# A retrieval kernel's second attention in two query groups, the second between the gathers; GpSimd adds a quarter of the gathered rows

## The reference

```python
# x: (512, 1024); ctx: (256, 1024); both normed and modulated -> h, hc; u = h @ w_in
q = rms_norm(u[:, :256]) @ w_uq                 # 16 heads of 64 + 32 (rotary) features
k, v = split(rms_norm([u; uc][:, 256:384]) @ w_ukv)   # 768 keys: 512 tokens + 256 of the context
y_a = softmax(q k^T * 96**-0.5) v @ w_o_mla
y_c = conformer_conv(u)                         # 31 taps, layer norm, silu, pointwise
x = x + g1 * ((gate_a * y_a + gate_c * y_c) @ w_out)
h2 = modulate(rms_norm(x), sh2, sc2)
# per token and each of 8 heads: top 16 of 128 x 128 experts by product keys
hidden = gelu(u_experts[e] . h2)                # e: 8 * 16 = 128 experts for each token
x = x + g2 * sum(gate * hidden * v_experts[e])
out = rms_norm(x)
```

## Time and profile before

| what | us |
|---|---|
| median of 3 runs | 3001.97 (2996.91 to 3003.27) |
| the profiled execution's own time | 3003.84 |
| its span in the profile | 3002.5 |
| TensorE busy | 2639.8 (88%) |
| VectorE busy | 1573.3 (52%) |
| ScalarE busy | 651.6 (22%) |
| GpSimd busy | 547.8 (18%) |
| bytes moved by DMA | 685.25 MB, 536.90 of them by the gathers' queue |

### The profile page before, as it was taken

How to read it: one execution, slowest core, us unless ns; L and a number is a source line. 1 busy time by engine, 2 the same in 40 slices (tenths; PEclk the granted TensorE clock), 3 DMA queues, 4 the chain that set the end, 5 groups by cost and what they waited for, 6 DMA issues and landing times.

```text
span 3002.5 us, 23370 instructions
## 1 busy us (share of the span) xinstructions
PE 2639.8 (88%) x8074; PEld 1387.7 (46%) x8074; DVE 1573.3 (52%) x3510; ACT 651.6 (22%) x1573; POOL 547.8 (18%) x523
## 2 busy tenths in 40 slices
PE   8998999999998999999999988889877777777776
PEld 3684446666444444356657533445432323232222
DVE  1106335443106991266634676647675676758554
ACT  2114220001001002156511112212121221222111
POOL 0000000000000000000001343334434434434332
PEclk9997899999999999999999998999999899999999
DMA  3220023343221221000236999999999999999997
GB/s 137 99 84 1 22 84 140 140 168 128 90 77 64 84 79 49 14 1 1 81 117 253 380 377 384 398 392 411 411 419 404 387 420 420 420 420 420 420 420 313
DMA packets 87156, 685.25 MB, mean 228 GB/s; under 512 B 9960, under 2 KB 10600, under 8 KB 12800
## 3 DMA queue, kind: packets, MB, share of 16 engines
q0 software_dynamic: 73728, 536.90, 44.0%
q1 hardware_dynamic: 11264, 141.82, 12.4%
q10 hardware_dynamic: 2048, 5.03, 0.5%
HBM read 681.62 MB, written 2.10 MB: 228 GB/s over the span
## 4 chain that ended last, share of the span: by engine, by line
PE 64%; DMA 23%; DVE 8%; ACT 3%; issue 1%; POOL 0%; ACTq 0%; DVEq 0%
PE psum L345 34%; DMA weights<-in_experts,expert 12%; PE psum L896 12%; DMA slot<-in_experts,expert 11%; PE psum L829 3%; PE psum L738 3%; PE psum L683 2%; PE psum L796 2%; DVE slot L1835 2%; PE psum L760 1%; DVE weights L1835 1%; PE psum L811 1%; PE psum L746 1%; ACT spare_row L1292 1%; PE psum L519 1%
## 5 line engine op out<-in xcount | busy, mean ns | idle before, releaser
L896 PE MATMUL psum<-slot,spare_row 128*128 128x512 f32 x1096 | 518.6, 618 | 123.0 <-ACT spare_row L1292 120.6
L896 PE MATMUL psum<-weights,spare_row 128*128 128x512 f32 x952 | 457.2, 625 | 152.4 <-ACT spare_row L1292 145.8
L1835 DVE CUSTOM_DVE_ANT_0 slot<-slot,hT 128x1024 f32<-128x1024 f32 x274 | 333.6, 1222 | 198.2 <-DMA slot<-in_experts,expert 196.6
L345 PE MATMUL psum<-xnT,weights 128*128 128x257 f32 (+2 forms) x1568 | 423.8, 432 | 2.8 <-DVE xnT L1341 2.8
L896 PEld LDWEIGHTS psum<-slot,spare_row 128*128 128x128 f32 x1096 | 207.0, 196 | 410.9 <-issue 211.9
L1889 POOL DMA_INDIRECT weights<-in_experts,expert x238 | 253.2, 1064 | 767.6 <-PE psum L896 399.2
L1835 DVE CUSTOM_DVE_ANT_0 weights<-weights,hT 128x1024 f32<-128x1024 f32 x238 | 290.0, 1223 | 182.8 <-DMA weights<-in_experts,expert 181.8
L896 PEld LDWEIGHTS psum<-weights,spare_row 128*128 128x128 f32 x952 | 180.1, 198 | 416.9 <-ACT spare_row L1292 215.1
L1889 POOL DMA_INDIRECT slot<-in_experts,expert x274 | 291.4, 1064 | 418.6 <-PE psum L896 404.0
L345 PEld LDWEIGHTS psum<-xnT,weights 128*128 128x128 f32 x1568 | 298.8, 191 | 118.5 <-issue 82.2
L1287 ACT ACTIVATE coef<-hidden 128x2 f32<-128x2 f32 (+1 forms) x257 | 52.2, 203 | 1004.5 <-DVE hidden L1835 1004.5
(11 more groups left out here) (320 smaller groups left out, 2534.0 us busy)
## 6 DMA issues: line engine op xcount, KB each, us to landing
weights<-in_w_mod SPq DMA_DIRECT2D x12, 2048.0 KB, 8.7
weights<-in_w_up SPq DMA_DIRECT2D x11, 2048.0 KB, 7.7
weights<-in_w_in SPq DMA_DIRECT2D x8, 2048.0 KB, 8.7
weights<-in_w_pq SPq DMA_DIRECT2D x8, 2048.0 KB, 10.4
weights<-in_w_out SPq DMA_DIRECT2D x6, 2048.0 KB, 8.7
weights<-in_w_in_t SPq DMA_DIRECT2D x4, 2048.0 KB, 10.7
weights<-in_w_down SPq DMA_DIRECT2D x4, 2048.0 KB, 7.8
weights<-in_w_o_mla SPq DMA_DIRECT2D x4, 2048.0 KB, 8.7
```

Of the source, the lines that this page charges most:

```text
L345: last = pe.matmul(out, lhsT, rhs, start=start and n == 0, stop=stop and n == len(pairs) - 1)
L896: last = pe.matmul(acc.pair[:, half, :], k.diags[pick % 8], k.slots[slot][:, D + half * 512:D + (half + 1) * 512], start=h0 == 0 and j == ...
L1835: ins = dve.tensor_tensor_reduce(slot[:, 0:D], slot[:, 0:D], k.h2[:, i, :], 1.0, 0.0, ALU.mult, ALU.add, hid[:, j:j + 1])
```

## The change

The second attention is split by queries: `attention(0)` (tiles 0 and 1, 32 items) stays where it was, `attention(1)` (tiles 2 and 3, 32 items) becomes the head of `late` and is issued between the picks, one step a group, with one idle step after every odd item (`breath`). Both groups read `w_uq` and `w_ukv` again; `w_uq` has 512 more columns, so that the swapped rotary part comes from a second projection in place of the swap matmul. Keys are computed once in each group, value rows by head pair in each group (`value_rows`). Uses of PSUM in the attention and of the accumulators come out of fixed bank pairs (`among`): in `attention(1)` the scores have pair 2, the transposes pair 3, queries, keys and values pair 1 alone. To make room, four blocks of 1.05 MB (x, gates, merged branch and modulation rows of the later half) and one of 0.52 MB are written to DRAM (`hold`, on ScalarE's queue) and read back (`back`, on SP's) before `dense(1)`. `dense` has half as many, larger steps. Of the picks of tiles 0 and 1 every odd one, except in the last 16 of the tile, is added by GpSimd (112 of 256): ScalarE multiplies the second half of its slot by the coefficient in place, GpSimd adds it to a sum in SBUF, and one identity matmul a tile adds that sum to the accumulator.

The diff's core (the rest renames tiles, places them in memory and numbers the counts):

```diff
 class Kernel:
+    def by_pool(self, pick):
+        return pick < 2 * PH * TOPK and pick % 2 == 1 and pick % (PH * TOPK) < PH * TOPK - 16
+    def breath(self, g, c):
+        return range(g * (c % 2))
     def lagging(self, steps):
         return chained(range(2), steps)
 # tensor_program
-    def attention():
-        unit_q, wq = weights(2, 1536)
+    def attention(g):
+        my, items = k.work[g], k.heads_order[g]
+        for_scores, for_turned, for_rest = (((0, 1), (2,), (3,)), ((2,), (3,), (1,)))[g]
+        unit_q, wq = weights(2, 2048)
         unit_kv, wkv = weights(1, 2048)
...
+        queries(0, range(4))
+        yield
+        keys(0)
+        yield
+        yield from k.gap(2)
+        for c in range(len(items) + 4):
+            if g and 0 <= c - 3 < len(items):
+                transposes(c - 3)
+            if c < len(items):
+                scores(c)
+                if c % 4 == 1 and h + 2 < AH:
+                    keys(h // 2 + 1)
+                if c % 4 == 2 and h // 4 + 1 < AH // 4:
+                    queries(h // 4 + 1, (0, 1) if c % 8 == 2 else (2, 3))
+            if g == 0 and 0 <= c - 3 < len(items):
+                transposes(c - 3)
+            if c >= 4 and c % 4 == 0:
+                value_rows(c // 4 - 1)
+            if c >= 4 and c % 4 == 3:
+                u = values((c - 4) // 4)
+            yield
+            yield from k.breath(g, c)
...
     def peer():
-        late = dense(1)
+        late = chained(attention(1), dense(1))
...
+                    if not k.by_pool(pick):
+                        pe.wait_ge(s.diag, n + 1)
...
                 next(late, None)
+            if last_batch and i < 2:
+                pe.wait_ge(*max(t for t in k.taken[:pick] if t[0] is s.pooled))
+                for half in range(2):
+                    last = pe.matmul(acc.pair[:, half, :], ident[:], k.sums[i][:, half * 512:(half + 1) * 512], start=False, stop=True)
 # scalar_program, attention(g)
+        for c in range(len(items) + 4):
+            if c < len(items):
+                exps(c)
+                if c % 4 == 1 and h + 2 < AH:
+                    keys(h // 2 + 1)
+                if c % 8 == 2 and h // 4 + 1 < AH // 4:
+                    queries(h // 4 + 1)
+            if 0 <= c - 3 < len(items):
+                transposes(c - 3)
+            if c >= 4 and c % 4 == 0:
+                value_rows(c // 4 - 1)
+            yield
+            yield from k.breath(g, c)
 # scalar_program, peer
+                    else:
+                        slot, loads, before = k.gathers[pick]
+                        row = k.slots[slot][:, D:2 * D]
+                        act.wait_ge(s.ld_slot[slot], 16 * loads)
+                        act.activation(row, row, ACT.Copy, scale=cf[:, j:j + 1]).then_inc(s.scaled)
 # gpsimd_program
             if before is not None:
-                pool.wait_ge(s.picked, before + 1)
+                if k.by_pool(before):
+                    add_row(before)
+                pool.wait_ge(*k.taken[before])
 # add_row
+            pool.tensor_tensor(k.sums[i][:], k.sums[i][:], row, ALU.add).then_inc(s.pooled)
 # sync_program
+        if g:
+            sp.wait_ge(*k.psum.of["q", 1, AH // 4 - 1, 3].free)
+            sp.wait_ge(*k.psum.of["a_v", 1, AH // 2 - 1].full[-1])
+            back("merged", s.hold_merged, s.back_merged)
+            back("sig", s.hold_sig, s.back_sig)
+            back("x", s.hold_x, s.back_x)
+            back("rows", s.hold_rows, s.back_rows)
```

More of the change, by code:

```diff
@@ L299, in memory @@
     k.g1, k.sh2, k.sc2, k.g2 = k.mod_rows
+    k.later["norm"] = k.sc2
     BH = PH // 2
@@ L335, in tensor_program, with take @@
     ident = k.ident
-    def take(key, reads=1, n=1):
-        u = ps.use(key, reads, n)
+    def take(key, reads=1, n=1, among=None):
+        u = ps.use(key, reads, n, among)
         for e in u.empty:
@@ L714, in queries @@
                 k.ring_done[unit_q] = u.full[-1]
[L715 to L717 removed]
         def keys(p):
[L720 removed]
+            u = take(("k", g, p), n=2, among=for_rest)
             for a in range(2):
[L722 removed]
+                last = chain(u.pair[:, a, 0:KH], [(wkv[:, 0, p * P:(p + 1) * P], my.ckv[:, a * KH:(a + 1) * KH])])
@@ L723, in keys, with value_rows @@
+            last.then_inc(u.fill())
+        def value_rows(p):
+            u = take(("v", g, p), n=2, among=for_rest)
+            for j in range(KT):
+                last = pe.matmul(u.pair[:, j // 3, (j % 3) * P:(j % 3 + 1) * P], my.ckv[:, j * P:(j + 1) * P], wkv[:, 0, D + p * P:D + (p + 1) * P],
+                                 start=True, stop=True)
             last.then_inc(u.fill())
@@ L747, in transposes, with values @@
             last.then_inc(u.fill())
[L749 to L756, removed]
+        def values(p):
+            V, PT = my.V[p % len(my.V)], my.probsT[p % len(my.probsT)]
+            u = take(("a_v", g, p), among=for_rest)
+            pe.wait_ge(*ps.of["v", g, p].free)
+            for c in range(4 * p, 4 * p + 4):
+                pe.wait_ge(*ps.of["a_t", g, c].free)
             for j in range(KT):
                 for a in range(2):
-                    rows = slice(a * VD, (a + 1) * VD)
-                    last = pe.matmul(u.pair[rows, 0, 0:2 * P], k.values[j][:, (2 * p + a) * VD:(2 * p + a + 1) * VD], k.probsT[q][:, j, a * 2 * P:(a + 1) * 2 * P],
+                    last = pe.matmul(u.pair[a * VD:(a + 1) * VD, 0, 0:PAIR], V[:, j, a * VD:(a + 1) * VD], PT[:, j, a * PAIR:(a + 1) * PAIR],
                                      start=j == 0, stop=j == KT - 1)
@@ L915, in tensor_program @@
     conv_out()
-    attention()
+    for _ in attention(0):
+        pass
     first_tile()
@@ L1159, in conv_out, with attention, queries @@
         feature_norm("n_ckv_c", [k.ckv[:, SEQ:NKV]], CTX, 128, 3, k.feature_root[2])
-    def attention():
-        act.wait_ge(*of["pw", KC - 1].free)
-        for j in range(KT):
-            u = of["values2", j]
-            for half in range(2):
-                act.wait_ge(*u.full[half])
-                ins = act.activation(k.values[j][:, half * 512:(half + 1) * 512], u.pair[:, half, :], ACT.Copy)
-            ins.then_inc(u.out)
-        def queries(g):
-            Q = k.Q[g % 2]
+    def attention(g):
+        my, items = k.work[g], k.heads_order[g]
+        if g == 0:
+            hold("merged", of["pw", KC - 1].free, s.hold_merged)
+        else:
+            act.wait_ge(s.hold_rows, 16)
+            act.wait_ge(s.hold_sig, 16)
+            act.wait_ge(s.merged, KC)
+            act.wait_ge(s.h2, 2)
+        def queries(q):
@@ L1278, in peer @@
     def peer():
-        late = k.lagging(dense(1))
-        pick = group = 0
+        late = k.lagging(chained(attention(1), dense(1)))
+        pick = group = n = 0
         for b, (i, h0, nh) in enumerate(k.order):
-            beside = k.beside(b, finish_tile, route)
+            beside = k.beside(b, 2, finish_tile, route)
             cf, hid = k.coef[b % 2], k.hidden[b % 2]
@@ L1600, in feature_norm, with query_norm @@
         ins.then_inc(s.feature)
+    def query_norm():
+        root = k.feature_root[0]
+        dve.wait_ge(*of["n_cq"].free)
+        dve.reciprocal(root[:], root[:]).then_inc(v.up())
+        dve.wait_ge(*v.now())
+        dve.wait_ge(s.hold_x, 16)
+        for x in range(2):
+            for g in range(2):
+                cut = slice(g * PAIR, (g + 1) * PAIR)
+                ins = dve.scalar_tensor_tensor(k.work[g].cq[:, x, :], k.cq[:, x, cut], col(k, "q_g", x), root[:, cut], ALU.mult, ALU.mult)
+        ins.then_inc(s.feature)
     def conv_out():
```

459 lines of the change are left out of this document (270 added, 189 removed).

## The result

The changed kernel takes **3210.15 us** (median of 4 runs, 3208.44 to 3214.98) against 3002.59 of the kernel before: a ratio of 1.0698, 95% interval 1.068 to 1.0717. It is slower, as forecast, but by 208 us where 29 were forecast, outside the stated range.

A forecast was written before the change was run, and what follows sets the result against it. The prediction took the attention as bound by TensorE and the gathers as bound by the DMA. From the profiled 3003.84 us, -92 (attention ahead), +121 (tiles 0 and 1) and 0 (tiles 2 and 3) gave 3033 us, range 2940 to 3105.

The forecast's parts named there:

- Term 1: Attention ahead of the picks: 142 us in place of 234.2, so the first gather starts 92 us earlier.
- Term 3: Tiles 2 and 3: stay with TensorE and the DMA at 420 GB/s, a change of 0.
- Term 2: Picks of tiles 0 and 1, with the moved attention beside them: 821 us in place of 700, +121 us.
- GpSimd then needs 4.8 us a group, just under the DMA's 5.: Tiles 0 and 1: two gather issues and an add of 2.2 us fit under the DMA's time per group.
- half an add on average in front of a dot: Tiles 0 and 1: 112 adds delay VectorE's dots by 1.1 us each, 123 us, half hidden under the DMA: +62.
- 7.2 us a group: Tiles 0 and 1 beside attention: TensorE's wait for ScalarE delays slot reuse, 21.6 us per three groups; 54 groups take 389 us.
- 391 us at 420 GB/s, 5.75 a group: The 68 groups behind the attention: DMA time for gathers, weights and data read back; 5.9 a group taken, 401 us.
- Table loads: ScalarE, attention beside picks: switching between exponential and Gelu costs a table load of about 1.3 us each way.
- A: Tiles 0 and 1: other gathers in flight hide TensorE's wait, 6.2 us a group with attention, 2969 us; chance 0.36.
- B: Tiles 0 and 1: GpSimd's adds and VectorE's dots block each other, +62 us, 3095 us; chance 0.18.
- The bounds 6.2 to 8.2 for a group: Tiles 0 and 1 with attention: limits around the forecast pace per group, 54 us either way.

The follow-up runs named there:

- experiments 1 and 2: The changed kernel with all GpSimd adds moved back to TensorE, 3100.83 us; the changed kernel with two zero-writing memsets in place of each add, 3111.6 us.
- a lag of one: The changed kernel with ScalarE and VectorE taking the late steps one group behind TensorE in place of two: 3163.61 us.
- spreading: Changed kernel without adds, late steps one group behind, gate multiply on ScalarE, second-group items without idle steps, dense steps with one: 3017.15 us.
- (7): The changed kernel without GpSimd's adds and with late steps one group behind TensorE in place of two: 3050.56 us.
- (12): The spreading kernel, with TensorE also issuing an item's scores ahead of the transposes: 3009.82 us.
- experiment 3: The kernel before, with 96 unneeded GpSimd adds of 128 x 1,024 behind every other gather from pick 320 on: 3071.54 us.

## Why the prediction was wrong

**Term 1 held.** 92 us forecast, 94 measured; the attention ahead of the picks ran from 1261 to 1401, 140 us against 142. **Term 3 held**: 662 us in both kernels.

**Term 2 failed**, 821 us forecast and 1005 measured: 420 against 520 with the attention, 401 against 485 behind it. Without the adds it was 465 and 430. So the adds make 110 of the 184 us, and the two sizes that were too low the rest, in these steps:

- *"GpSimd then needs 4.8 us a group, just under the DMA's 5."* The add was costed as GpSimd's own time, and the conflict with VectorE's two-operand instructions was put off to a rival with a chance of 0.18 and a price of 62 us. It is real (experiments 1 and 2), and the adds cost 109 us, 0.98 us each. The forecast kept it out of the sum because the trace before had no GpSimd instruction with two inputs. That trace did hold a sign of it, which was overlooked: of the gathers issued from 1600 to 2325 us, the 71 that began with more than 0.1 us of a dot left to run took 1.47 us on average and up to 1.98, and each ended 0.81 us behind the dot's end; the 127 that began while neither a dot nor a TENSOR_TENSOR ran took 0.94. In the changed kernel a multiplication of 0.16 us took 2.93 beside an add (2202.31 us); beside the memsets, which only write, the multiplications took 0.174 on average.
- *"half an add on average in front of a dot"*, the rival's own price, had the wrong victim. Behind each dot stands the gate multiplication, and behind that ScalarE, TensorE and the release of the slot. Of the 127 multiplications from 1540 to 2545 us, 40 lasted 2.9 to 3.0 us, 12 more 1.6 to 2.2, and 73 their 0.16. The 40 all begin 0.5 to 0.7 us ahead of the add's record, as at 2202.31 and 2209.38, and end with the add. So where the order brings the two together, it isn't half an add by chance but more than a whole one. Taking the multiplication off VectorE got some 40 us back.
- *"7.2 us a group"* for the attention's part, 7.0 with the six groups that have no item. It was 8.8 with the adds and 7.9 without, 8.1 with the memsets. The wait that the number was built on is there (168.9 us for ScalarE's copy) and a lag of one removed 47 to 50 us, so the mechanism was right. The size came out low, and why is open. One candidate is the clock: the step was worked with TensorE's durations from a part of the trace at a granted clock of 0.96 and more, while in this stretch the mean was 0.77, with TensorE idle 44% of the time. What the clock alone cost wasn't tried apart.
- *"391 us at 420 GB/s, 5.75 a group"*, and 5.9 taken, for the rest: it was 7.1 us a group with the adds and 6.3 without. The adds make 55 of the 84 us that the forecast lacks here. The remaining 29 us don't hang on the number of TensorE's picks: with the memsets TensorE has one pick less in most groups and is busy only 314 of 430 us, and without the adds it has them all, and both take 430 us. The DMA share is 0.96 and 0.95 in them, but at 373 GB/s, where the forecast reckoned with 420. The kernel before had 378 and 404 GB/s in the two parts of this stretch, at shares of 0.97 and 0.99: it came to a steady 420 only in tiles 2 and 3. Why the DMA moves less here at the same share wasn't tried. So the adds were meant against a bound that no version showed here, and put a costlier one in its place: 485 us.
- *Table loads*: counted in the wait, one load of 1.3 us in every three groups, which makes 23 us for 54 groups. They were worth 22 us with the adds and about 28 without. That step stood.

**The rivals.** A, that the overlap holds, needed 6.66 us a group or less. No version with the changed kernel's lag came near. With a lag of one, no adds, the gate on ScalarE and no table loads, the 59 groups took from 1540 to 1920, 6.4 us each, and the kernel was 7 us above the kernel before. B had the mechanism and the direction; its price of 62 us was too low, and it was set on a base that was too low as well. Its argument against itself, that GpSimd might fall in VectorE's reads of PSUM, carried little: only 8 of the 32 maxima of scores (L1758) met an add at all; they took 0.94 to 0.96 us, as the others did. The bounds 6.2 to 8.2 for a group left out the case in which both troubles come together, and so did the range's upper end of 3105: its cases were priced one at a time, while 3210 has both, 109 us for the adds and 97 us without them.

The account: 3210 - 109 (adds) - 50 (lag) - 12 (gate) - 21 (spreading) - 7 (scores first) = 3010, with the kernel before at 3003. The first two terms are clear of the noise; of the last three only the sum, from (7) to (12), is a gain beyond the intervals.

## What to carry to other kernels

Before GpSimd gets an elementwise job beside a busy VectorE, count VectorE's instructions with two SBUF operands, the smallest among them first: the one on which other engines wait was held up longest here (1.32 us on average for 0.16, 2060 to 2545 us; the dots 1.44 for 1.22). Then look at those with one operand, such as the division of an item (1.21 for 0.62 with a lag of one). Moving work behind a DMA-bound stage buys its length at the front only if the engine that does it has that much left over in the stage; here TensorE had 106 of 705 us left (599 busy, 1635 to 2340 us before) and was given 116 (715 busy in the last version). That this is the limit is my reading, not a tested one. And in a hand-interleaved order, draw who waits for whose step of which group before choosing a lag: one group too many cost 50 us.

## What the runs showed of the hardware

- GpSimd's add of 128 x 1,024 took 2.37 to 2.42 us on average in every group of rows, against 1.04 for a copy of the same size in the changed kernel (the other copy, in part beside other work, 1.21).
- A dot that met an add was recorded with up to 4 us (2605.25 in the kernel of experiment 3), a multiplication of 128 x 2 with 2.93. This dot's record, too, starts ahead of the add's, by 0.57 us, and it ends 1.1 us behind the add. The longer time counts as busy, so a page of busy shares shows a fuller VectorE and no wait (358 of 485 us in the changed kernel from 2060 us on, 251 of 430 without the adds from 2010 us on): the mean duration of an instruction that didn't change is what gives it away.

```profile
2605.25 4.01 DVE L1835 CUSTOM_DVE_ANT_0 weights<-weights,hT 128x1024 f32<-128x1024 f32 x1
2605.82 2.35 POOL L1896 TENSOR_TENSOR merged<-merged 128x1024 f32<-128x1024 f32 x1
2608.33 1.76 POOL L1889 DMA_INDIRECT slot<-in_experts,expert  x1 [0.16 <-PE psum L896]
2609.19 1.21 DVE L1835 CUSTOM_DVE_ANT_0 weights<-weights,hT 128x1024 f32<-128x1024 f32 x1
```

- The issue of an indirect gather was recorded longer where it began while a dot ran: 1.82 and 1.93 us in the changed kernel at 2201.03 and 2207.99, and in the kernel before 1.47 on average over the 71 cases above, against 0.94 where neither a dot nor a TENSOR_TENSOR ran at its start. The dots of those 71 kept their 1.22. One case of the kernel before, in which the issue ends at 2123.48 and the dot at 2122.67:

```profile
2121.44 1.23 DVE L1835 CUSTOM_DVE_ANT_0 slot<-slot,hT 128x1024 f32<-128x1024 f32 x1 [1.33 <-DMA slot<-in_experts,expert]
2121.55 1.93 POOL L1889 DMA_INDIRECT weights<-in_experts,expert  x1 [2.22 <-PE psum L896]
```

No run isolated this.
